# Expert layers in four 64 by 64 tiles of the array, with second buffers in the front of the kernel and a new load order in the state stage

## The reference

```python
def block(hb):                       # 128 tokens at a time; 8 heads, 16 experts for each token and head
    q = (hb @ w_q).reshape(128, 8, 2, 256)
    s = einsum("nhkd,hkmd->nhkm", q, sub_keys)
    ...                              # the best 16 of 16 x 16 candidate sums give ids and weights g
    ue, ve = take(u_tab, ids), take(v_tab, ids)
    act = gelu(einsum("nd,nhkd->nhk", hb, ue))
    return einsum("nhk,nhkd->nd", g * act, ve)

# state-space mixer: powers of a complex a for each of 64 groups x 64 states, a scan over the tokens
a_r, a_i = mag * cos(li * step), mag * sin(li * step)
h = scan(a, bb @ u);  y = c_r @ h_r - c_i @ h_i
```

## Time and profile before

| | |
|---|---|
| time, median of 3 runs | 3750.82 us (3746.65 to 3755.1) |
| the profiled execution: its time | 3749.29 us |
| its span | 3747.4 us |
| mean granted TensorE clock | 0.934 of full |
| PE, DVE, ACT, POOL busy | 3166.1, 2247.1, 1429.8, 962.4 us |
| transferred | 1152.67 MB, mean 308 GB/s |
| of it by the gathers' queue | 827.38 MB, 53.9% of 16 engines' span |

### The profile page before, as it was taken

How to read it: one execution, slowest core, us unless ns; L and a number is a source line. 1 busy time by engine, 2 the same in 40 slices (tenths; PEclk the granted TensorE clock), 3 DMA queues, 4 the chain that set the end, 5 groups by cost and what they waited for, 6 DMA issues and landing times. The chain is left out here.

```text
span 3747.4 us, 46785 instructions
## 1 busy us (share of the span) xinstructions
PE 3166.1 (84%) x15952; PEld 2087.9 (56%) x15952; DVE 2247.1 (60%) x5038; ACT 1429.8 (38%) x3564; POOL 962.4 (26%) x796
## 2 busy tenths in 40 slices
PE   3886999999988999897766798888877989889897
PEld 2774566554444655442345644444326779777897
DVE  5664766667667666679414466767752259512397
ACT  1222444434334444443224244444432237423275
POOL 0001433434333333344200155444550000000000
PEclk7887999999999999999977899999998989899999
DMA  6746999999999999999967499999992235332353
GB/s 248 277 167 267 418 415 417 421 419 409 421 420 399 409 405 415 415 417 352 369 230 238 163 421 421 421 421 415 415 406 106 90 130 179 135 115 91 129 183 118
DMA packets 177136, 1152.67 MB, mean 308 GB/s; under 512 B 21860, under 2 KB 30264, under 8 KB 43306
## 3 DMA queue, kind: packets, MB, share of 16 engines
q0 software_dynamic: 113936, 827.38, 53.9%
q1 hardware_dynamic: 56058, 304.90, 21.6%
q10 hardware_dynamic: 6944, 17.91, 1.3%
HBM read 1128.86 MB, written 21.25 MB: 307 GB/s over the span
## 5 line engine op out<-in xcount | busy, mean ns | idle before, releaser
L1126 PE MATMUL PS<-AR 128*128 128x512 f32 x3072 | 1511.9, 618 | 249.6 <-ACT AR L1184 241.7
L1311 POOL DMA_INDIRECT AR<-in_peer_uv,AR x768 | 949.2, 1236 | 1514.0 <-PE PS L1126 1109.2
L1287 DVE CUSTOM_DVE_ANT_0 AR<-AR,H 128x1024 f32<-128x1024 f32 x768 | 940.9, 1225 | 655.9 <-DMA AR<-in_peer_uv,AR 636.2
L1126 PEld LDWEIGHTS PS<-AR 128*128 128x128 f32 x3072 | 559.8, 193 | 852.9 <-issue 420.4
L1179 ACT ACTIVATE SM<-SM 128x1 f32<-128x1 f32 x768 | 155.7, 203 | 1130.4 <-DVE SM L1287 1125.3
L1087 PEld LDWEIGHTS PS<-HT,W 128*128 128x128 f32 x1536 | 298.9, 195 | 273.2 <-issue 258.0
L1087 PE MATMUL PS<-HT,W 128*128 128x256 f32 x1536 | 427.6, 387 | 2.7 <-issue 1.3
L1184 ACT ACTIVATE AR<-CON,SM 128x128 f32<-128x128 f32 x768 | 309.1, 402 | 45.6 <-PE PS L1126 21.1
L2578 PE MATMUL PS<-XP,WP 128*128 128x256 f32 x2112 | 264.2, 287 | 22.5 <-DVE WP L2735 15.4
L2578 PEld LDWEIGHTS PS<-XP,WP 128*128 128x128 f32 x2112 | 261.0, 196 | 28.2 <-issue 27.7
L1181 ACT ACTIVATE SM<-SM 128x1 f32<-128x1 f32 x768 | 227.1, 296 | 25.1
(11 more groups left out here) (368 smaller groups left out, 3313.0 us busy)
## 6 DMA issues: line engine op xcount, KB each, us to landing
W<-in_peer_w_q SPq DMA_DIRECT2D x48, 1024.0 KB
W<-in_ada_w SPq DMA_DIRECT2D x32, 1024.0 KB
W<-in_ffn_gate SPq DMA_DIRECT2D x22, 1024.0 KB
W<-in_ffn_val SPq DMA_DIRECT2D x22, 1024.0 KB
W<-in_ffn_out SPq DMA_DIRECT2D x22, 1024.0 KB
W<-in_cm_w_in SPq DMA_DIRECT2D x16, 1024.0 KB
AR<-min_scr SPq DMA_DIRECT2D x16, 1024.0 KB, 9.6
AR<-in_peer_uv,AR POOLq DMA_INDIRECT x768
```

The lines of the kernel that those rows point to most:

```text
L1126: mm = pe.matmul(PS[:, 4 + (u % 2) * 2 + c, :], self.DIAG[:, r % 4, :], self.UV[:, r % RING, D + c * 512:D + (c + 1) * 512], start=(k == 0 ...
L1287: v.tensor_tensor_reduce(rows_, rows_, H[:, self.tb(u), :], 1.0, 0.0, ALU.mult, ALU.add, self.ACTV[:, u % 2, k:k + 1]).then_inc(u_used.sem, 1)
L1311: g.indirect_dma_start(out=self.UV[:, r % RING, :], out_offset=None, in_=t["peer_uv"], in_offset=bass.IndirectOffsetOnAxis(ap=self.IDS[:, ...
```

## The change

It has three parts.

**Tiles.** `DIAG` becomes 128 by 64: the two diagonal blocks of the old matrix, one below the other, made from `EYES` (two 64 by 64 identities). PE runs four matmuls for a row in place of two. Each takes one half of the tokens (64 rows) and 512 columns of v, and writes 64 partitions: rows 0 to 63 or 64 to 127 of the array, columns 0 to 63 or 64 to 127. Column half c of the result now lies in partitions c * 64 and up, and the half of the tokens picks the PSUM bank. `add_rows` brings this back to token order with four operations of 64 by 512.

**Front.** `MOUT` gets a second buffer, placed where `peer0` keeps its scores, so ACT waits for the seventh store before `peer0`. The end of `dve_powers` becomes `dve_powers_of`, with `ada0[0].add_bias()` between the two. `act_roots` moves ahead of the fifth block of the mixer, and the counts of `some` change.

**Order.** In the x state stage `load_chunk` runs two chunks ahead of `load_matrices`, and the lags of the first three output chunks are loaded between them.

```diff
-                self.MOUT = view(0, 2, CG, T8 * GDIM)
+                self.MOUT = [view(18432, 2, CG, T8 * GDIM), view(0, 2, CG, T8 * GDIM)]
...
-                    if c:
-                        v.wait_ge(self.mout_out, c * 16)
+                    if c > 1:
+                        v.wait_ge(self.mout_out, (c - 1) * 16)
...
-            DIAG = view(20224, 4, P)
+            HP = P // 2
+            DIAG, EYES = view(20224, 4, HP), view(20480, HP)
...
-                    for c in range(2):
-                        mm = pe.matmul(PS[:, 4 + (u % 2) * 2 + c, :], self.DIAG[:, r % 4, :], self.UV[:, r % RING, D + c * 512:D + (c + 1) * 512],
-                                       start=(k == 0), stop=(k == TOPK - 1))
+                    for x in range(2):
+                        for half in range(2):
+                            c, rows_ = (half + x) % 2, slice(half * self.HP, (half + 1) * self.HP)
+                            mm = pe.matmul(PS[c * self.HP:(c + 1) * self.HP, 4 + (u % 2) * 2 + half, :], self.DIAG[rows_, r % 4, :],
+                                           self.UV[rows_, r % RING, D + c * 512:D + (c + 1) * 512], start=(k == 0), stop=(k == TOPK - 1))
...
-                        a.mul(self.DIAG[:, r % 4, :], IDENT, self.WGT[:, u % 2, k:k + 1]).then_inc(diag_ready.sem, 1)
+                        a.mul(self.DIAG[:, r % 4, :], self.EYES, self.WGT[:, u % 2, k:k + 1]).then_inc(diag_ready.sem, 1)
...
-                sums = PS[:, 4 + (u % 2) * 2:6 + (u % 2) * 2, :].rearrange("p a b -> p (a b)")
-                dve.link(v, v.tensor_tensor(self.YG, sums, gate, ALU.mult))
+                for i in range(2):
+                    for c in range(2):
+                        out, here, cols = slice(i * self.HP, (i + 1) * self.HP), slice(c * self.HP, (c + 1) * self.HP), slice(c * 512, (c + 1) * 512)
+                        one = v.tensor_tensor(self.YG[out, cols], PS[here, 4 + (u % 2) * 2 + i, :], gate[here, cols], ALU.mult)
+                dve.link(v, one)
...
-            for c in range(2):
+            for c in range(4):
                 statex.load_chunk(c)
             for c in range(2, NCH):
-                statex.load_chunk(c)
                 statex.load_matrices(c)
-            for c in range(3):
-                outs.load_lags(c)
+                if c + 2 < NCH:
+                    statex.load_chunk(c + 2)
+                if c > 4:
+                    outs.load_lags(c - 5)
...
             mixc.act_squares()
+            mixc.act_roots()
             drain(mixc.act_in(4))
             matrices(2)
-            mixc.act_roots()
...
+            prep.dve_powers()
             ada0[0].add_bias()
-            prep.dve_powers()
+            prep.dve_powers_of()
```

More of the change, by code:

```diff
@@ L834, in act_store @@
                 a.wait_ge(self.mout_done, c + 1)
-                a.dma_start(mout_scr[c], self.MOUT.rearrange("p r g x -> p (r g x)")).then_inc(self.mout_out, 16)
+                if c:
+                    a.wait_ge(self.mout_out, c * 16)
+                a.dma_start(mout_scr[c], self.MOUT[c % 2].rearrange("p r g x -> p (r g x)")).then_inc(self.mout_out, 16)
                 a.wait_ge(self.k_saved, c + 1)
@@ L920, in dve_powers, with dve_powers_of @@
                 drain(self.cmul(self.BBR, self.BBI, over_c(self.CO_R), over_c(self.CO_I), self.BR, self.BI, self.T1, self.T2))
+            def dve_powers_of(self):
+                L, X1, X2, A_R, A_I, PR, PI = self.link, self.X1, self.X2, self.A_R, self.A_I, self.PR, self.PI
                 L(v.memset(PR[:, 0], 1.0))
@@ L953, in dve @@
                 for c in range(NCH):
-                    MIN, CST, MOUT = self.MIN[c % 2], self.CST[c % 2], self.MOUT
+                    MIN, CST, MOUT = self.MIN[c % 2], self.CST[c % 2], self.MOUT[c % 2]
                     if c > 1:
@@ L1276, in dve @@
                     drain(self.choose(u))
+                for i in range(2):
+                    half = slice(i * self.HP, (i + 1) * self.HP)
+                    dve.link(v, v.tensor_copy(self.EYES[half], IDENT[half, half]))
                 self.gates(0)
@@ L2200, in first_block_norm @@
                 yield from normd.roots((0,))
+            a.wait_ge(prep.mout_out, 7 * 16)
             peer0.act(fill_act(), rest_of_matrices, first_block_norm())
@@ L2256, in first_dve @@
             drain(norm1c.apply())
-            some(40)
+            some(42)
             ada0[1].add_bias()
             mixc.dve_means()
-            some(2)
+            some(1)
             mixc.dve_vars()
-            some(2)
+            some(1)
             drain(mixc.dve_apply(0))
-            some(24)
+            some(30)
             ada0[2].add_bias()
-            some(6)
+            some(4)
             drain(mixc.dve_mix())
```

## The result

The changed kernel takes 3719.18 us (median of 4 runs, 3715.22 to 3724.3). The kernel before took 3752.37 us (4 runs) beside it: ratio 0.9916, 95% interval 0.99 to 0.9932. By the ratio that is 31.5 us less (26 to 38), and gains are given so from here on; the two medians differ by 33. The forecast was 3703, its range 3680 to 3735. It is faster, as forecast, by two thirds of the gain.

A forecast was written before the change was run, and what follows sets the result against it. The prediction took a DMA ceiling of some 422 GB/s, not PE, to bound the expert layers, and waits elsewhere. Terms -25 -18 -10 -2 +5 +1 = -49, rounded to -47, gave 3703 us, range 3680 to 3735.

The forecast's parts named there:

- The front, -25: Front, ahead of the gathers: three waits fall and the expert layer moves up whole, 25 us off; bounds 8.5 and 32.
- the powers' 8.5 us: Front: the first part of the powers runs while DVE waited for PE's rows; everything behind moves up 8.5 us.
- the hole's 10: Front: PE's 10.45 us idle before the fourth chunk's turns shrinks, with roots earlier and two MOUT buffers; 10 us off.
- the lower clock's 7: Front: after that idle time PE ran at 1.2 GHz, costing 7.8 us, of which 7 should return.
- PE's part, -10 and -2: Expert layers: faster rows recover time below the rate ceiling, 10 us in the first (bounds 0 and 25), 2 in the second.
- DVE's part, +5: DVE bound stretch around 1690 to 1790 us: four operations replace one in some four units, 5 us more (2 to 15).
- The x state stage, -18: X state stage: inputs no longer wait behind matrices, the scan begins near 1939 and the rest follows; 18 us off.
- My lower bound of 6 us: X state stage: the gain if matrices and late weights ahead make inputs land no sooner in all rounds but one.
- (a): Front or x state stage gives only its lower bound: 3715 to 3719 us, with both 3731; chance 0.17.
- (b): Expert layers: only two of four tiles run together, heavy row 3.41 us, time 3792; with all one by one, chance 0.08.
- (c): Expert layers: PE, less busy, gets the lower clock, a row without fill takes 3.0 us, time 3741; chance 0.05.
- (d): Whole kernel: the change does nothing outside PE's busy time, other waits eat the gains, 3745 to 3752 us; chance 0.04.

The follow-up runs named there:

- e9: The changed kernel with two tiles for all units: each half of the rows writes its own half of the sums, DVE moves them once; 3764.96 us.
- e12: The changed kernel with the powers back in one piece behind the bias of the first rows; 3732.83 us.
- e7: The changed kernel with DVE taking the sums in one 128 by 1024 operation, half landing in wrong places, four tiles kept; 3715.65 us.
- e10: The changed kernel with two tiles and one move by DVE in the last four units of each expert layer only; 3723.28 us.
- e5: The changed kernel with PE taking the late stage's ada rows one chunk later, behind the next chunk's states; 3720.75 us.
- e6: The changed kernel loading only the first half of each block of the late stage's ada weights, so the second norm's modulation differs; 3713.13 us.
- e11: The kernel before, with its old load order, loading only the first half of each block of the late stage's ada weights; 3741.29 us.
- e4: The changed kernel with the old matmuls, diagonals and single move of the sums, keeping the new front and load order; 3724.84 us.

## Why the prediction was right in sign and size of the front, and too high in the rest

**The whole.** The forecast's terms were -49 us, the pair of traces has -29.0. Of the 20 us between them the x state stage has 12.1 (-18 forecast, -5.9 measured) and the tiles 7.8 (-10 -2 +5 +1 forecast, +1.8 measured in the first layer and nothing in the second). The front gave 0.8 more than forecast, and the stretches between and behind the stages lost 0.9.

**The bound.** That faster matmuls give little under a full DMA queue was right: PE's busy time fell by 312 us and the first layer did not get shorter. e9 is the counter-check: a heavy row takes 3.36 us in place of 3.01, PE is busy 96% of the first window in place of 91%, and the layer grows by 43 us.

**The front, -25.** It gave 25.8 us in the profiled pair; over all kernels the first gather moved from 329.3 (four) to 305.7 (nine), 23.6 us. The parts are seen in the traces: the powers' 8.5 us as 7.8 at the first product and 8.6 ahead of the hole (e12, the powers alone: 8.9 at the first product, 11 at the gathers), the hole's 10 as 10.5, the lower clock's 7 as 7.8. The size came out of three terms that each came true, less 1.1 us.

**PE's part, -10 and -2: the first step that was mis-sized.** It measured -4.6 us (old form 1531.2, e7 1526.6) and nothing in the second layer. I took 422 GB/s as what every stretch could reach and gave PE ten of the 29 us that two windows lacked; the windows after reach 418 and 410 with PE at 78%. What they still lack is not PE's.

**DVE's part, +5.** It measured +6.1 in the first layer, inside its bounds of 2 to 15. The mechanism was that of the forecast, but only some 2.5 us of it lie at the end of the layer where I had put it (e10). Part lies at the change of streams, which I had not named, so the close number is partly luck. Together the tiles cost 1.5 us in the layer, not -5.

**The x state stage, -18: the step that failed.** The forecast was that the scan "begins near 1939. The rest hangs on it", from chunk 6 landing 18 us sooner with 15 us a load. The landing came 14.1 us sooner and the scan 12.6; and the rest did not hang on it, as the scan then lasted 6.7 us longer. The sum had put nothing for that. Before, the last ada rows ran 6 us into the scan (1963.20), so most of its first half had no weights to wait for: these windows of before and of changed show what it moved into (the same columns as above).

```profile
1956.00:1976.00 20.00, 13.03 (x328) 9.38 (x328) 17.40 (x89) 10.41 (x17) 0.00 (x0) 0.76 0.55 146
```

```profile
1911.00:1931.00 20.00, 10.87 (x186) 7.57 (x185) 9.86 (x48) 7.81 (x12) 1.05 (x2) 0.63 1.03 320
1931.00:1951.00 20.00, 9.66 (x172) 6.56 (x172) 14.07 (x72) 8.81 (x13) 0.00 (x0) 0.59 0.96 359
```

The first 20 us of the scan had a DMA share of 0.55 before; now the window in which it starts has 1.03 and the next one, which ends 32 us into it, 0.96. There PE waits for weights and DVE for PE. Asking in another order on PE brought a later landing of the matrices and no shorter stage (e5). Fewer bytes brought earlier landings and took 10 to 11 us off the stage, in either order (e6, e11). Which loads give way to which inside the full stretch was not run apart. My lower bound of 6 us, "if the matrices and `late`'s weights ahead of them make the inputs land no sooner in all rounds but one", had the right culprit and nearly the right size, but through the inputs; it came in through what the later chunks wait for, the weights in the changed kernel and the matrices in e5. With chunk 6 landing 14 us sooner, that the bound met the size is luck.

**The rivals.** (a) is what happened, for the x state stage alone: it put 3715, measured 3719, the rest being the tiles. (b) didn't: rows are short. Of (c) the first half came true and the price didn't. The granted clock fell from 0.97 to 0.91 and 0.87 in the first layer's long windows, from 0.99 to 0.85 in the second layer and from 0.95 to 0.60 where DVE is the bound, but PE still stood idle 41 of 100 us there, and no layer grew by it. (d) is refuted by the front. Of the signs for the profile after, the scan's first copy came 14.0 us closer to the end of the expert layer (97.6 to 83.6 us behind SP's load of the step sizes), not 18; the others came true, but for a rate of 410 and 341 GB/s in two windows.

What is left open: the hole and the lower clock are told apart by places in one pair of traces, and by no run of their own. Of DVE's 6.1 us e10 shows 2.5 at the end, and the rest is put at the change of streams by one pair of windows. What stops PE in the middle of its ada rows is not known.

## What to carry to other kernels

Where the DMA share is 1.0 in a stretch, a load that is issued sooner takes the place of another: here the scan began 12.6 us sooner and lasted 6.7 longer. Before counting on an earlier landing, add up the bytes of everything that must be in by the end of the stretch. A faster matmul form under a full queue is worth the few stretches in which the rate falls, and any work that it moves to another engine must be priced in exactly these stretches, at the change of phases too. With a spread of 10 us between runs, distances between fixed points in a trace can tell apart effects of 2 us that the whole time can't, but only in a stage that repeats so well: the first expert layer did (1.3 us), the front (12) and the x state stage (4.5) didn't.

## What the runs showed that was not expected

Four tiles of 64 by 64 ran eight float32 matmuls of 512 columns in 1.02 us in two orders, two diagonal tiles the same eight in 1.86, and the full array four in 1.71: so four tiles give 1.7 times, not 2, and with the 0.19 us more on the work between rows 1.4 times.

The same front, in nine kernels, ended between 298.7 and 311.1 us. PE's granted clock goes with it. The windows 76 to 196 and 196 to 300 us, of the changed kernel and then of e6:

```profile
76.00:196.00 120.00, 104.23 (x1414) 92.36 (x1413) 95.66 (x119) 25.79 (x38) 0.53 (x1) 0.94 0.71 270
196.00:300.00 104.00, 86.16 (x411) 76.08 (x411) 59.98 (x127) 20.62 (x35) 1.57 (x3) 0.79 0.44 163
```

```profile
76.00:196.00 120.00, 108.45 (x1402) 94.97 (x1400) 93.75 (x112) 24.30 (x35) 0.53 (x1) 0.90 0.70 269
196.00:300.00 104.00, 82.88 (x396) 74.30 (x396) 54.96 (x103) 21.62 (x36) 1.57 (x3) 0.76 0.39 143
```

At 0.94 and 0.79 the first gather stands at 302.4, at 0.90 and 0.76 at 311.1. Over the nine kernels the six that begin their gathers by 306.8 have 0.92 to 0.94 in the first of these windows, and the three later ones (e4, e7, e6) 0.90 or 0.91. PE is busy 87 and 83% of the two windows in the changed kernel, so this is where the whole times of like kernels part by some us, and why e4 against changed says less than the table. What makes the clock differ in identical code these traces don't tell.
